# A two-layer hybrid decoder step on one core: nine of 44 projection pairs by one level of Strassen's scheme, with a ring of four weight buffers

## What is computed

```python
h = rms_norm(x, norm_mix[l])
z = h @ w_in[l]                       # one projection of 11288 columns: q, k, v, gates of all three mixers
o_a = windowed softmax attention      # three groups of 8 heads, window and dilation (128,1) (512,4) (2048,16)
o_b = gated linear attention          # 4 heads, state 64 x 128, chunks of 64 tokens
o_c = gated DeltaNet                  # 4 heads, state 128 x 128, convolution of width 4
merged = sum of sigmoid(gate) * (o_a, o_b, o_c) @ w_branch[l]
x = x + merged @ w_out[l]
h = rms_norm(x, norm_ffn[l])
x = x + (silu(h @ w_gate) * (h @ w_up)) @ w_down      # layer 0, 2816 wide; layer 1: top 2 of 8 experts, 1792 wide
```

## Time and profile before

| | |
|---|---|
| median of three runs (lowest, highest) | 1804.47 us (1804.31, 1809.21) |
| span of the profiled execution, first to last instruction | 1802.1 us |
| TensorE products, busy | 1748.8 us, 97% |
| VectorE / ScalarE / GpSimd, busy | 41% / 20% / 9% |
| mean granted TensorE clock, share of full | 0.993 |
| layer 0: projections begin, feed-forward block begins | 24.6 us, 565.1 us |
| layer 1: projections begin | 784.8 us |
| moved by the transfer engines | 563.96 MB, 313 GB/s mean |

### The profile page before, as it was taken

How to read it: one execution, slowest core, us unless ns; L and a number is a source line. 1 busy time by engine, 2 the same in 40 slices (tenths; PEclk the granted TensorE clock), 3 DMA queues, 4 the chain that set the end, 5 groups by cost and what they waited for, 6 DMA issues and landing times.

```text
span 1802.1 us, 30183 instructions
## 1 busy us (share of the span) xinstructions
PE 1748.8 (97%) x12542; PEld 1282.9 (71%) x12542; DVE 743.5 (41%) x1548; ACT 364.3 (20%) x760; POOL 154.3 (9%) x259
## 2 busy tenths in 40 slices
PE   9999999999999999999999998999989999999997
PEld 7889888787768999978898887877663343333423
DVE  3444542434535765534544414355342332233222
ACT  2241333433101000012313333331011110100001
POOL 3000000403200111000100002032000000000000
PEclk9999999999999999999999999999999999999999
DMA  9833599999999997899535899899958999999994
GB/s 296 285 120 100 187 324 316 359 310 367 388 347 392 365 321 286 288 348 371 194 107 207 308 325 346 312 350 384 333 211 327 393 377 414 402 398 394 371 415 177
DMA packets 265853, 563.96 MB, mean 313 GB/s; under 512 B 14654, under 2 KB 163362, under 8 KB 265441
## 3 DMA queue, kind: packets, MB, share of 16 engines
q1 hardware_dynamic: 246384, 500.15, 76.8%
q0 software_dynamic: 18544, 58.58, 9.2%
q10 hardware_dynamic: 784, 3.26, 0.5%
HBM read 547.75 MB, written 196.63 MB: 413 GB/s over the span
## 4 chain that ended last, share of the span: by engine, by line
PE 85%; SPq 7%; DMA 4%; DVE 2%; issue 1%; ACT 1%; DVEq 0%; POOL 0%; ACTq 0%; POOLq 0%
PE PS L940 34%; PE PS L1598 8%; PE PS L1374 8%; SPq L811 7%; PE PS L1350 5%; PE PS L1382 4%; PE PS L859 3%; PE PS L986 3%; PE PS L1576 3%; PE PS L1364 2%; PE PS L979 2%; PE PS L1636 2%; PE PS L1321 1%; PE PS L1537 1%; DMA mem<-bias_tables 1%
## 5 line engine op out<-in xcount | busy, mean ns | idle before, releaser
L940 PE MATMUL PS<-h,mem 128*128 128x264 f32 x2816 | 654.3, 389 | 0.0
L940 PEld LDWEIGHTS PS<-h,mem 128*128 128x128 f32 x2816 | 527.8, 191 | 106.7 <-issue 21.3
L1806 ACT COPY z<-PS 128x264 f32<-128x264 f32 (+5 forms) x293 | 119.5, 430 | 737.6 <-PE PS L940 527.6
L1598 PE MATMUL PS<-mem,z 128*32 128x512 f32 (+1 forms) x1536 | 146.1, 523 | 3.8 <-DMA mem<-in_moe_w_up 3.8
L2893 DVE COPY small<-mem 128x1024 f32 x56 | 38.8, 693 | 175.6 <-PE PS L1576 117.8
L1598 PEld LDWEIGHTS PS<-mem,z 128*32 128x32 f32 x1536 | 47.4, 110 | 77.8 <-issue 61.2
L1576 PE MATMUL PS<-small,z 128*32 128x256 f32 (+2 forms) x624 | 86.9, 396 | 1.3 <-DVE z L2893 1.3
L1350 PE MATMUL PS<-z,mem 128*128 128x264 f32 x384 | 87.3, 388 | 0.0
L1576 PE MATMUL PS<-z 128*32 128x256 f32 (+2 forms) x624 | 87.0, 396 | 0.0
L1350 PEld LDWEIGHTS PS<-z,mem 128*128 128x128 f32 x384 | 72.3, 190 | 13.8 <-issue 1.7
L1374 PE MATMUL PS<-z,mem 128*128 128x132 f32 x624 | 78.3, 278 | 0.0
(11 more groups left out here) (377 smaller groups left out, 2028.2 us busy)
## 6 DMA issues: line engine op xcount, KB each, us to landing
out_win_s<-in_cache_win_kv SPq DMA_DIRECT2D x128, 1023.5 KB, 11.9
mem<-in_w_in SPq DMA_DIRECT2D x88, 1024.0 KB, 7.6
mem<-in_moe_w_gate SPq DMA_DIRECT2D x80, 512.0 KB, 9.7
mem<-in_moe_w_up SPq DMA_DIRECT2D x80, 512.0 KB, 8.9
mem<-in_moe_w_down SPq DMA_DIRECT2D x64, 512.0 KB, 13.6
out_win_s<-in_cache_win_kv SPq DMA_DIRECT2D x32, 1022.0 KB, 13.1
z<-in_moe_w_down SPq DMA_DIRECT2D x48, 512.0 KB, 13.1
z<-in_moe_w_up SPq DMA_DIRECT2D x32, 512.0 KB, 10.6
```

The costliest lines, as they stand in the source:

```text
L940: last = mm(bank(l, "p", j)[:, 0:T], w[:, k, P * (j % 2):P * (j % 2) + P], h[:, k, :], start=(k == 0), stop=(k == KT - 1))
L1598: last = mm(m_bank("c", "gu", g, b, w, r)[BLK * j:BLK * j + BLK, 0:n], hs[:, k, P * r + BLK * j:P * r + BLK * j + BLK], v3(slot_ap(set_slo ...
L1806: return nc.scalar.copy(out, in_)
```

## The change

Nine pairs of each layer, 23 to 31 (tiles 46 to 63, the last six of the keys and all of the values), are computed by the seven products of blocks. The even tile of a pair becomes the steps fold_x and fold_y (16 products of 132 columns), the odd one fold_x2 and fold_y2 (12), in banks 0 and 1, which the tiles had by turns. fold_h, once a layer behind small_turn, makes four sums of the input on VectorE. fold_w makes the four sums of one chunk's weights on GpSimd, one of them in place; it stands one pair ahead in the list. From pair 25 to 29 it waits until pair q-2 is computed, whose buffers it takes; for 30 and 31 it waits for the stores of both states. VectorE puts the results together out of the two banks, ScalarE copies a quarter of each. The fold steps have no drain ahead of them.

The ring of the projection, branch and output chunks has four buffers; the fifth one's place (and 64 columns more) holds the sums of the input. The memory behind it moves by 64 columns. The ring of seven keeps its buffers. The semaphores fw_odd, fw_even and hd_ready count the new sums too, and the waits of the feed-forward block are raised accordingly. Two buffers of the linear attention's sample step (qz_s, gqs) move to another place of the same memory. GpSimd waits in kv_tok, ahead of the bias tables, until pair 29 is computed.

```diff
-RING = 5
+RING, BASE = 4, 5
...
+HALF = T // 2
+UNSETTLED = ("proj", "fold_x", "fold_y", "fold_x2", "fold_y2", "fold_w")
+FOLD = tuple(range(23, 32))
...
+    def tile(j):
+        q = j // 2
+        if q not in FOLD:
+            return [("proj", j)]
+        return [("fold_x2", q), ("fold_y2", q)] if j % 2 else [("fold_x", q), ("fold_y", q)]
...
+    s += p() + [("small_turn",), ("fold_h",)] + p(2) + [("conv_v", 0)] + p() + [("gate_c",)] + p() + [("conv_v", 1)]
...
-        return [step, ("proj_half", j), (step[0] + "2", *step[1:]), ("proj", j)]
+        first, rest = tile(j) if j // 2 in FOLD else (("proj_half", j), ("proj", j))
+        return [step, first, (step[0] + "2", *step[1:]), rest]
...
+    for q in FOLD:
+        before = ("fold_x", q - 1) if q - 1 in FOLD else ("proj", 2 * q - 2)
+        s.insert(s.index(before) + 1, ("fold_w", q))
...
+        fold_t = mem[:, RING * CW:RING * CW + 4 * 4 * HALF].rearrange("p (n k t) -> p n k t", n=4, k=4)
...
+        FIXED = dict(par=0, ab=1, xn=2, fold_x=0, fold_x2=0, fold_y=1, fold_y2=1)
...
+                place(n0 + q, q % RING, (l, "fold_y2", q) if q in FOLD else (l, "p", 2 * q + 1))
+            held[BASE - 1] = (l, "fold_y2", FOLD[-1])
...
+        def fold_set(q):
+
+            return (S_G0 if q >= 30 else S_LA if q >= Z_K // 2 else S_K0) + q % 2
+
+        def fold_before(q):
+
+            same = [r for r in FOLD if r < q and fold_set(r) == fold_set(q)]
+            return same[-1] if same else None
...
+            def four(out, left, right, opens=False):
+
+                for k in range(4):
+                    last = mm(out, left[:, k, :], right[:, k, :], start=(opens and k == 0), stop=(k == 3), skip_group_check=True)
+                return last
+
+            def fold_x(l, q):
+                wait_chunk(pe, CH0[l] + q)
+                open_bank(pe, l, "fold_x", q)
+                x_ = bank(l, "fold_x", q)
+                four(x_[:, 0:HALF], fold_quarters(l, q)[0], h[:, 0:4, 0:HALF], True)
+                pe.wait_ge(hd_ready, h_sum(l, 3))
+                pe.wait_ge(fw_even, even_sum(l, q, 1))
+                four(x_[:, HALF:T], fold_sums(q)[1], fold_t[:, 1]).then_inc(full(l, "fold_x", q), 1)
+
+            def fold_y(l, q):
+                pe.wait_ge(fw_odd, odd_sum(l, q))
+                open_bank(pe, l, "fold_y", q)
+                y_ = bank(l, "fold_y", q)
+                four(y_[:, 0:HALF], fold_sums(q)[0], fold_t[:, 0], True)
+                four(y_[:, HALF:T], fold_quarters(l, q)[2], fold_t[:, 2]).then_inc(full(l, "fold_y", q), 1)
+
+            def fold_x2(l, q):
+                open_bank(pe, l, "fold_x2", q)
+                four(bank(l, "fold_x2", q)[:, 0:HALF], fold_quarters(l, q)[1], h[:, 4:8, 0:HALF]).then_inc(
+                    full(l, "fold_x2", q), 1)
+
+            def fold_y2(l, q):
+                open_bank(pe, l, "fold_y2", q)
+                y_ = bank(l, "fold_y2", q)
+                four(y_[:, HALF:T], fold_quarters(l, q)[3], fold_t[:, 3])
+                pe.wait_ge(fw_even, even_sum(l, q, 2))
+                four(y_[:, 0:HALF], fold_sums(q)[2], h[:, 4:8, HALF:T]).then_inc(full(l, "fold_y2", q), 1)

...
+            def fold_x2(l, q):
+                wait_full(act, l, "fold_x2", q)
+                copy(fold_out(q)[:, 0:HALF], bank(l, "fold_x2", q)[:, 0:HALF]).then_inc(free(l, "fold_x2", q), 1)
...
+            def fold_h(l):
+                h11, h12, h21, h22 = h[:, 0:4, 0:HALF], h[:, 0:4, HALF:T], h[:, 4:8, 0:HALF], h[:, 4:8, HALF:T]
+                tt(fold_t[:, 0], h12, h11, SUB)
+                tt(fold_t[:, 2], h22, h12, SUB).then_inc(hd_ready, 1)
+                dve.wait_ge(hd_ready, h_sum(l, 1))
+                tt(fold_t[:, 1], h22, fold_t[:, 0], SUB).then_inc(hd_ready, 1)
+                dve.wait_ge(hd_ready, h_sum(l, 2))
+                tt(fold_t[:, 3], h21, fold_t[:, 1], SUB).then_inc(hd_ready, 1)
+
+            def fold_x(l, q):
+                if q != FOLD[0]:
+                    wait_read(dve, l, "fold_y2", FOLD[FOLD.index(q) - 1])
+                wait_full(dve, l, "fold_x", q)
+                nc.vector.tensor_reduce(fold_ve[:, 0, :], bank(l, "fold_x", q)[:, 0:T].rearrange("p (w t) -> p t w", w=2),
+                                        AX.X, ADD).then_inc(free(l, "fold_x", q), 1)
+
+            def fold_y(l, q):
+                wait_full(dve, l, "fold_y", q)
+                nc.vector.tensor_reduce(fold_ve[:, 1, :], bank(l, "fold_y", q)[:, 0:T].rearrange("p (w t) -> p t w", w=2),
+                                        AX.X, ADD).then_inc(free(l, "fold_y", q), 1)
+                wait_read(dve, l, "fold_x", q)
+                wait_read(dve, l, "fold_y", q)
+                tt(fold_out(q)[:, 3 * HALF:4 * HALF], fold_ve[:, 0, :], fold_ve[:, 1, :], ADD)
+
+            def fold_y2(l, q):
+                wait_full(dve, l, "fold_y2", q)
+                tt(v3(fold_out(q)[:, HALF:3 * HALF], 2), v3(bank(l, "fold_y2", q)[:, 0:T], 2),
+                   bc(fold_ve[:, 0, :], 1, [P, 2, HALF]), ADD).then_inc(free(l, "fold_y2", q), 1)

...
+            def fold_w(l, q):
+                wait_chunk(pool, CH0[l] + q)
+                if fold_before(q) is not None:
+                    wait_full(pool, l, "fold_y2", fold_before(q))
+                elif fold_set(q) in (S_LA, S_SIG):
+                    pool.wait_ge(sems["eb_ready"], V("eb_ready", l))
+                    pool.wait_ge(sems["ke_ready"], V("ke_ready", l))
+                elif fold_set(q) in (S_G0, S_G1):
+                    pool.wait_ge(stored["gdns"], 16 * (l + 1))
+                    pool.wait_ge(stored["glas"], 32 * (l + 1))
+                tt = nc.gpsimd.tensor_tensor
+                a11, a12, a21, a22 = fold_quarters(l, q)
+                s1, s2, s4 = fold_sums(q)
+                tt(s1, a21, a22, ALU.add)
+                tt(a21, a11, a21, ALU.subtract).then_inc(fw_odd, 1)
+                pool.wait_ge(fw_odd, odd_sum(l, q))
+                tt(s2, a22, a21, ALU.subtract).then_inc(fw_even, 1)
+                pool.wait_ge(fw_even, even_sum(l, q, 1))
+                tt(s4, a12, s2, ALU.subtract).then_inc(fw_even, 1)
+
...
+                wait_full(pool, l, "fold_y2", 29)
```

91 lines of the change are left out of this document (58 added, 33 removed).

## The result

The changed kernel takes 1820.85 us (median of 4 runs, 1818.43 to 1824.26), the kernel before in the same session 1804.39 us (4 runs, 1801.65 to 1809.21): a ratio of 1.009 (95% interval 1.0066 to 1.0113), 16.5 us slower. I had forecast 1802.1 us, and a range up to 1809.5. The profiled execution has a span of 1818.0 us against 1802.1, so the two traces hold 15.9 of the 16.5 us.

A forecast was written before the change was run, and what follows sets the result against it. TensorE, busy 1748.8 of 1802.1 us, was taken as the bound. 1802.1 - 13.1 + 2.5 + 8.2 = 1799.7 us of span, plus 2.4 us around it, gave 1802.1 us; 8-in-10 range 1796.5 to 1809.5.

The forecast's parts named there:

- Term 1: Projection pairs on TensorE: 28 short products replace 16, 0.82 us gained a pair, 16 pairs count, 13.1 us less.
- pair 31 gains nothing: Last pair, behind the last norm: its tiles end earlier, but TensorE only waits longer for the bias tables.
- Term 2: GpSimd's weight sums beside VectorE's steps: ten meetings at 0.25 us each, 2.5 us more.
- Rival 2: VectorE and GpSimd exclude each other: half a sum for ten meetings, 6.0 us, 1805.6 us in all; chance 0.25.
- Term 3: Ring of four buffers: free except at layer 0's end, where a late feed-forward chunk costs 8.2 us more.
- Three pairs ahead are enough for that: free: Chunk loads in the ring of four: issued three pairs ahead, about 19 us, costing nothing, 2 us at worst.
- The late feed-forward chunk: End of layer 0: second feed-forward chunk, issued behind the last output tile, lands 7.3 to 10.8 us later; 8.2 taken.
- The sums of h and of the results: VectorE's input sums cost nothing; result sums 0 to 0.2 us a pair, pair 31's 1.2 us wait hidden under the bias wait.
- The sign: Whole kernel against a 0.3% (5.4 us) threshold: same 0.65, slower 0.2, faster 0.15.
- rival 3: GpSimd and VectorE exclude each other at full price: 12 us for ten meetings, 1811.6 us, slower; chance 0.1.

The follow-up runs named there:

- e13: e10 with eight pairs, 23 to 30, and pair 31 an ordinary projection again: 1798.39 us, 0.9962 of before.
- e12: e10 with GpSimd's sums of weights shrunk to one element each, TensorE reading the chunk's own quarters instead (tiles 46 to 63 come out wrong): 1787.72 us, 0.9908.
- e9: Kernel before, cache copies moved: none behind chunks 48 to 50, three behind 24 to 27, two behind the last four feed-forward chunks: 1795.34 us, 0.9933.
- e10: Changed kernel with nine pairs, ring of five outside projection tiles 30 to 63, cache copies moved as in e9: 1798.49 us, 0.996 of before.
- e1: Kernel before with a ring of four mixer buffers and no pairs: 1824.11 us, 1.0122 of before.
- e3: Changed kernel, ring of four kept, feed-forward chunks in exchanged buffers so chunks 0 and 1 load behind wo tiles 1 and 3: 1820.0 us, 1.0088.
- e4: Changed kernel, ring of four kept, no cache copies behind chunks 48 and 49, three instead of two behind 24 to 27: 1801.84 us, 0.9988.
- e2: Changed kernel, nine pairs, ring of five outside projection tile 33 to pair 31, sums of h moved ahead of the first state step: 1811.27 us, 1.0041.
- e5: Kernel before, copies moved: three behind chunks 24 to 35, none behind 48 to 57 (layer 0) or 48 and 49 (layer 1): 1806.65 us, 1.0025.
- e7: Changed kernel, ring of four, feed-forward chunks in e3's buffers, cache copies moved as in e5: 1816.01 us, 1.0086 of before.
- e14: e10 with the four sums of weights of each pair on VectorE instead of GpSimd: 1810.81 us, 1.0021 of before.
- e15: e14 with a pair's sums moved behind the second reduction of the pair before: 1798.16 us, 0.9961 of before.

## Why the prediction was wrong

**Term 1, the pairs' products: right.** Forecast 0.82 us a pair, 6.6 us a layer up to the last norm. Without the sums the stretch is 6.3 us shorter in each layer. That pair 31 gains nothing fits e13, which can't tell it from a gain of 1.6 us. What the prediction missed is that some of this is given back behind the norm: the bias tables land 10.19 and 9.81 us after issue in the two layers of e12, 8.19 and 9.16 in e9, and column *caches* is 1.0 and 1.3 us longer in e12.

**Term 2, GpSimd beside VectorE: right mechanism, wrong size.** Forecast 2.5 us for both layers, with rivals at 6 and 12. Against e12's 85.3 us the pairs' stretches are 2.5 and 2.3 us longer in the kernel after (4.8) and 3.2 and 2.5 in e10 (5.7). Rival 2 was the nearest, in size and in mechanism: the engine that comes second waits for the end of the other's operation. I had a price of 0.25 us a meeting from rows where VectorE reads PSUM, which turned out to be a kind of operation that meets nothing; that was the nearest row but not the same resource. The meetings are also more than the ten norm steps that I counted: the 0.30 us addition of two sums is 138 ns longer on average over nine, and TensorE's wait at the state step, after which the granted clock fell to half in some traces, was not in the sum at all.

**Term 3, the ring: the step that failed.** Forecast 8.2 us; the ring alone costs 21.4 (e1). The step that failed is "Three pairs ahead are enough for that: free": the term priced one late chunk, and put the value caches and the start at nothing. They cost 11.4 and 2.0 us in the kernel after. Three parts:
- The late feed-forward chunk: 7.3 to 10.8 us later was the bound, 10.4 was measured, and by the path that was forecast: issued behind the last output tile, landing 7.51 us later. The size taken, 8.2, was 2.2 too low. But a second cause stood behind the first. With the buffer set right (e3) SyncE still comes late, since copies ahead of the load hold it for 11.39 and 12.10 us. I had counted the loads' own issue times from the earlier trace rows and not what stands between them in the same queue.
- The value caches, 6.1 and 5.3 us: not in the prediction. I wrote that apart from the end of layer 0 three pairs ahead are enough, and looked only at the chunks themselves. TensorE waits there not for a weight but for GpSimd's loads, which take 18.70 us with copies of SyncE issued beside them. e1 shows that the ring alone brings this about, e4 that without these copies the wait is gone. How the ring does it is not shown: that the two copies now go out within 1.36 us instead of 7.76 was my explanation, but in e2 the first of them alone is held for 17.82 us and the loads take as long.
- The start, 2.0 us: in the text as "2 us at worst", and put at nothing. I had judged it by layer 1's first chunks, where there is indeed no loss (column state of layer 1: +0.5). In layer 0 a chunk takes 23.32 us.

**The sums of h and of the results: right.** Where they stood at first they cost nothing that shows, and pair 31's wait for its reduction was 1.14 us, forecast 1.2, under the bias wait.

**The balance.** 15.9 us of span = 2.0 (start) - 7.8 (pairs, sums included) + 1.6 - 1.6 (attention of the two layers) + 16.5 (caches and feed-forward chunk) + 0.5 + 5.3 (caches of layer 1) - 0.6. By my terms it was -13.1 + 2.5 + 8.2. By totals the single edits give ring 21.4, sums 9.4, pairs without sums -4.5 (ratios 0.9908 of e12 and 0.9933 of e9), 26 together; with intervals of some 8, 5 and 6 us either way that is not clear of 16.5. The clock shifts such sums as well: e1 and the kernel after both run the attention scores of layer 1 at full clock, where the kernel before has a granted clock of 0.83 and 0.60 at 1094 to 1106 us.

**The sign.** Slower by over 0.3% had a chance of 0.2, half of it from rival 3. It came mostly from costs that no rival named.

## What to carry to other kernels

A buffer less in a ring shifts the issue time of every transfer behind it. List what stands beside each of them, on the same engine's queue and on the others', and not only whether the ring's own data comes in time; the largest loss here fell on transfers that the change doesn't name. Background copies are worth more than their bytes: moved away from two places they brought the kernel before 0.67% (e9), to which nine Strassen pairs added nothing that the intervals can tell (e10), and put in a third place they took it back (e5). Before work goes to GpSimd, look at the operands of what VectorE does at that time: with two in SBUF each meeting cost up to a whole operation here, with PSUM operands nothing.

## What the runs showed of the hardware

- Issue time on SyncE depends on what is under way: one cache copy took 0.59 us to issue at 566.70 in the kernel after, 12.10 us in e3 and, at 489.29 us in e2, 17.82 us. In that time nothing behind it on SyncE goes out.
- GpSimd's sum of 512 columns takes 1.27 us alone, 2.29 us when two of VectorE's operations from SBUF surround it; VectorE's step of 1056 columns 1.32 and up to 2.45 us (e7, at 1080.32); its addition of 132 columns 0.30 and up to 1.42 us (the kernel after, at 306.49). Without GpSimd's sums (e12, e14, e15) the longest are 1.32 and 0.30 us.
- A wait of 0.5 us of TensorE in a stretch of small matmuls left the granted clock at 1.00 in one kernel and was followed by 0.51 in another; stretches at 0.50 appeared in untouched parts, too, 4 us (e10, at 22 us) and over 20 us long (e15, behind the router). The spread among runs of one kernel goes with the mean clock: e15's 14 us between fastest and slowest with 0.993 and 0.987.
